# Second products of a routed feed-forward layer: 192 tokens as the moving side, the last 64 tokens summed from fetched rows

## The reference

```python
q = (xi @ w_query).reshape(B, T, PEER_HEADS, 2, PEER_HALF)
s = jnp.einsum('bthcd,cnd->bthcn', q, sub_keys)
s_top, i_top = lax.top_k(s, PEER_TOPK)          # 16 of 128, twice per head
...                                             # 16 best of the 256 pairs, softmax -> gate, idx
u = u_tab[idx]
h = gelu(einsum('bthk,btd->bthk', u, xi))
w = gate * h
return jnp.einsum('bthk,bthkd->btd', w, v_tab[idx])
```

## Time and profile before

| | |
|---|---|
| median of 3 runs | 2190.05 us (2189.86 to 2190.96) |
| the profiled execution | 2193.35 us, span 2191.6 us |
| TensorE (PE) busy | 2158.0 us, 98% |
| VectorE (DVE), ScalarE (ACT), POOL busy | 71%, 57%, 32% |
| memory read | 371.96 MB, 170 GB/s over the span |

### The profile page before, as it was taken

How to read it: one execution, slowest core, us unless ns; L and a number is a source line. 1 busy time by engine, 2 the same in 40 slices (tenths; PEclk the granted TensorE clock), 3 DMA queues, 4 the chain that set the end, 5 groups by cost and what they waited for, 6 DMA issues and landing times. The chain is left out here.

```text
span 2191.6 us, 35588 instructions
## 1 busy us (share of the span) xinstructions
PE 2158.0 (98%) x13179; PEld 1882.8 (86%) x13179; DVE 1558.1 (71%) x2948; ACT 1250.2 (57%) x2471; POOL 704.0 (32%) x344
## 2 busy tenths in 40 slices
PE   8899999999999999999999999999999999999999
PEld 8789998888888888887999888888888889897888
DVE  8558978888666666665698778866666668457776
ACT  6444567777554545564446777755555455555443
POOL 2217977777100000001698777730000004100000
PEclk9899999999999999999999999999999999999999
DMA  5144555555566665553555555556666656434554
GB/s 173 48 156 155 193 173 165 164 170 164 187 193 193 195 194 192 167 169 104 179 187 183 168 166 165 164 182 192 192 193 194 195 168 221 135 108 166 189 192 153
DMA packets 122956, 375.34 MB, mean 171 GB/s; under 512 B 13200, under 2 KB 18064, under 8 KB 122784
## 3 DMA queue, kind: packets, MB, share of 16 engines
q1 hardware_dynamic: 122496, 373.05, 52.8%
q10 hardware_dynamic: 288, 0.01, 0.0%
HBM read 371.96 MB, written 1.05 MB: 170 GB/s over the span
## 5 line engine op out<-in xcount | busy, mean ns | idle before, releaser
L250 ACT ACTIVATE hi<-raw 128x1024 fp32r<-128x1024 f32 (+2 forms) x705 | 738.0, 1048 | 361.4 <-PE bank L1439 114.1
L259 DVE TENSOR_TENSOR lo<-raw,hi 128x1024 fp32r<-128x1024 f32 (+2 forms) x449 | 544.5, 1216 | 262.1 <-ACT hi L250 261.6
L259 POOL TENSOR_TENSOR lo<-raw,hi 128x1024 fp32r<-128x1024 f32 x256 | 620.4, 2428 | 212.3 <-ACT hi L250 212.0
L1480 PE MATMUL bank<-hi,pe_mh 128*128 128x512 f32 x1016 | 395.7, 389 | 1.3 <-DVE pe_ml L1734 1.3
L1481 PE MATMUL bank<-hi,pe_ml 128*128 128x512 f32 x1016 | 395.3, 389 | 0.0
L1428 PE MATMUL bank<-xx,hi 128*128 128x512 f32 x1176 | 308.9, 401 | 0.0
L1593 ACT ACTIVATE pe_mh<-pe_hidden 128x256 fp32r<-128x256 f32 x256 | 106.9, 418 | 342.0 <-PE bank L1487 342.0
L342 POOL TENSOR_TENSOR rstd<-mean,minus_half 128x2 f32<-128x2 f32 x6 | 4.2, 704 | 902.9 <-DVE mean L335 902.9
L1439 PEld LDWEIGHTS bank<-xx,lo 128*128 128x128 f32 x2048 | 270.3, 189 | 14.0
L1439 PE MATMUL bank<-xx,lo 128*128 128x256 f32 x2048 | 281.4, 280 | 0.0
L1487 PE MATMUL bank<-lo,pe_mh 128*128 128x512 f32 x1016 | 271.5, 389 | 0.0
(11 more groups left out here) (418 smaller groups left out, 3408.6 us busy)
## 6 DMA issues: line engine op xcount, KB each, us to landing
raw<-in_peer_u SPq DMA_DIRECT2D x256, 512.0 KB, 3.3
raw<-in_peer_v SPq DMA_DIRECT2D x256, 512.0 KB, 4.3
raw<-in_w_gate_up SPq DMA_DIRECT2D x44, 512.0 KB, 3.6
raw<-in_w_in SPq DMA_DIRECT2D x34, 512.0 KB, 4.2
raw<-in_gla_w_in SPq DMA_DIRECT2D x24, 512.0 KB, 3.6
raw<-in_w_down SPq DMA_DIRECT2D x22, 512.0 KB, 3.4
raw<-in_w_query SPq DMA_DIRECT2D x16, 512.0 KB, 3.3
raw<-in_mla_w_o SPq DMA_DIRECT2D x8, 512.0 KB, 3.3
```

Source lines behind the costliest of these rows:

```text
L250: act.activation(k.hi[:, n % RING, at_hi:at_hi + x * e], k.raw[:, n % RAW, 0:x * e], ACT.Copy).then_inc(k.hi_done, 1)
L259: eng.tensor_tensor(k.lo[:, n % RING, at_lo:at_lo + x * e], k.raw[:, n % RAW, 0:x * e], k.hi[:, n % RING, at_hi:at_hi + x * e].bitcast(F32 ...
L1480: pe.matmul(second_ps(a, c), mh[:, v % 2, tok], hi[:, r, half], start=(v == 0), stop=False)
```

## The change

The 256 tokens are split: the first 192 (`TD`) go on as before through streamed slabs, the last 64 (`TS`) get their second weights by indirect fetch.

For the 192, the second products are turned. The slab is now the array's weights, 128 columns at a time, and the middle values move: for each of eight 128-wide pieces of the width, one product of 384 columns (high and low part of 192 tokens, side by side in `middle`) with the slab's high part, and one of 192 columns with its low part. The sums come out as width by tokens in all eight banks. At the end of the stage ScalarE takes each bank's low half out, VectorE adds it to the high half, TensorE transposes the sums back (16 transposes), and only then are they added to `h`.

For the 64, ScalarE writes their function values to `stage`, which SyncE stores to a table in memory (`aside`, 16 stores of 256 KB). VectorE's ranking also computes for each of their 128 picks the expert's row and the place in `aside`. In the second stage a token has two partitions, with 64 picks each. POOL issues two indirect fetches for a pick: 128 single values of `aside` (`seen`) and 128 rows of 4 KB of the second weights (`found`, four places). VectorE multiplies value and gate and adds the scaled rows to `sums_aside`, in the steps of `PICK_AT` (steps 10 to 108, 64 of them), and merges the two halves at step 115. The streams of both weight tables stay whole.

The groups for the gates are 48 instead of 64, at `LEAD + g * 7 // 5`. Some semaphores are shared under new names.

```diff
@@ -1271,7 +1271,13 @@
 
 
 GROUP = 4
-GROUPS = T // GROUP
+TS = 64
+TD = T - TS
+ASIDE = P // TS
+PICKS = SLOTS // ASIDE
+STAGED = 8
+FOUND = 4
+GROUPS = TD // GROUP
...
-    return LEAD + g * 5 // 4
-
-
+    return LEAD + g * 7 // 5
...
 V_ORDER = ((0, 0), (1, 0), (0, 1), (1, 1))
+V_BANK = (4, 5, 6, 7, 3, 2, 0, 1)
+PICK_AT = {10 + n * 25 // 16: n for n in range(PICKS)}
+MERGE_AT = 115
 GROUP_AT = {slab_of(g): g for g in range(GROUPS)}
...
                 for c in range(2):
                     sp.dma_start(keys[c * 64:(c + 1) * 64, c * NK:(c + 1) * NK],
                                  k.dram["sub_keys"][l, :, c, :]).then_inc(keyed.sem, 16)
+
+                def put_aside(b):
+
+                    sp.wait_ge(bent.sem, bent.at(STAGED * b + STAGED))
+                    sp.dma_start(aside[:, STAGED * b:STAGED * (b + 1), :], stage[:, b % 2])\
+                        .then_inc(written[b % 2].sem, 16)
+
+                def place_picks():
+
+                    sp.wait_ge(ranked.sem, ranked.at(2))
+                    for g in range(ASIDE):
+                        sp.dma_start(picks[g * TS:(g + 1) * TS], packed[P - TS:P, :, g * PICKS:(g + 1) * PICKS])\
+                            .then_inc(placed.sem, 16)
+
                 for n in range(s0 + AHEAD, end + AHEAD):
                     load_slab(k, sp, n)
+                    i = n - u0 - STAGED
+                    if i == TURN + 2:
+                        place_picks()
+                    if 0 <= i < NK and i % STAGED == STAGED - 1:
+                        put_aside(i // STAGED)
 
...
@@ -1468,39 +1523,50 @@
                                              start=(hot is hot_h), stop=(hot is hot_l))
                     last.then_inc(summed.sem, 1)
 
+                def high(v, c):
+
+                    cols = hi[:, (v0 + v) % RING, c * P:(c + 1) * P]
+                    pe.matmul(k.bank[V_BANK[c]][:, 0:2 * TD], cols, middle[:, v % 2].rearrange("p s t -> p (s t)"),
+                              start=(v == 0), stop=False, skip_group_check=True)
+
+                def low(v, c):
+
+                    return pe.matmul(low_sum(c), lo[:, (v0 + v) % RING, SKEW + c * P:SKEW + (c + 1) * P],
+                                     middle[:, v % 2, 0], start=False, stop=(v == NK - 1), skip_group_check=True)
+
                 def second(v):
 
-                    r = (v0 + v) % RING
                     pe.wait_ge(m_lo.sem, m_lo.at(v + 1))
                     pe.wait_ge(k.hi_done, v0 + v + 1)
-                    for c in range(2):
-                        half = slice(c * 512, (c + 1) * 512)
-                        for a in range(NT):
-                            tok = slice(a * P, (a + 1) * P)
-                            pe.matmul(second_ps(a, c), mh[:, v % 2, tok], hi[:, r, half], start=(v == 0), stop=False)
-                            pe.matmul(second_ps(a, c), ml[:, v % 2, tok], hi[:, r, half], start=False, stop=False)
-                    pe.wait_ge(*k.lo_at[v0 + v])
-                    for c in range(2):
-                        half = slice(c * 512, (c + 1) * 512)
-                        for a in range(NT):
-                            tok = slice(a * P, (a + 1) * P)
-                            last = pe.matmul(second_ps(a, c), mh[:, v % 2, tok], lo[:, r, half], start=False,
-                                             stop=(v == NK - 1))
+                    for part in (range(0, 5), range(5, KD)) if v == 0 else (range(KD),):
+                        for c in part:
+                            if v == 0 and V_BANK[c] < 3:
+                                pe.wait_ge(gated.sem, gated_before(NK - 1 - (NK - 1 - V_BANK[c]) % 3))
+                            high(v, c)
+                        pe.wait_ge(*k.lo_at[v0 + v])
+                        for c in part:
+                            last = low(v, c)
                     last.then_inc(k.eaten, 1)
 
                 def last_second():
 
                     v = NK - 1
-                    r = (v0 + v) % RING
                     pe.wait_ge(m_lo.sem, m_lo.at(v + 1))
                     pe.wait_ge(k.hi_done, v0 + v + 1)
                     pe.wait_ge(*k.lo_at[v0 + v])
-                    for n, (a, c) in enumerate(V_ORDER):
-                        half, tok = slice(c * 512, (c + 1) * 512), slice(a * P, (a + 1) * P)
-                        pe.matmul(second_ps(a, c), mh[:, v % 2, tok], hi[:, r, half], start=False, stop=False)
-                        pe.matmul(second_ps(a, c), ml[:, v % 2, tok], hi[:, r, half], start=False, stop=False)
-                        pe.matmul(second_ps(a, c), mh[:, v % 2, tok], lo[:, r, half], start=False, stop=True)\
-                          .then_inc((first_part.sem if n < 3 else k.eaten), 1)
+                    for c in range(KD):
+                        high(v, c)
+                        low(v, c).then_inc((joined.sem if c < KD - 1 else k.eaten), 1)
+
...
+
+                    for a, half in V_ORDER:
+                        pe.wait_ge(added.sem, added.at(4 * half + 4))
+                        tok = slice(a * P, min((a + 1) * P, TD))
+                        for x in range(4):
+                            last = pe.transpose(second_ps(a, half)[0:tok.stop - tok.start, x * P:(x + 1) * P],
+                                                sums_t[:, 4 * half + x, tok], k.ident[:])
+                        last.then_inc(returned.sem, 1)
 
...
+                turn_back()
...
+                pool.wait_ge(placed.sem, placed.at(16 * ASIDE))
+                for x in range(2):
+                    pool.wait_ge(written[x].sem, written[x].at(8 * NK // STAGED))
+                for n in range(PICKS):
+                    if n >= FOUND:
+                        pool.wait_ge(mixed.sem, mixed.at(n - FOUND + 1))
+                    pool.indirect_dma_start(seen[:, n:n + 1], None, aside.rearrange("j i t -> (j i t)").unsqueeze(1),
+                                            bass.IndirectOffsetOnAxis(ap=picks[:, 1, n:n + 1], axis=0))\
+                        .then_inc(picked[n % FOUND].sem, 16)
+                    pool.indirect_dma_start(found[:, n % FOUND], None, v_rows,
+                                            bass.IndirectOffsetOnAxis(ap=picks[:, 0, n:n + 1], axis=0),
+                                            element_offset=l * NK * NK * D)\
+                        .then_inc(picked[n % FOUND].sem, 16)
+                pool.wait_ge(mixed.sem, mixed.at(PICKS))
+                for g in range(ASIDE - 1):
+                    pool.dma_start(others[P - TS:P, g * D:(g + 1) * D], sums_aside[g * TS:(g + 1) * TS])\
+                        .then_inc(merged.sem, 16)
                 after.roots(pool)
...
+                    b = i // STAGED
+                    if b >= 2 and i % STAGED == 0:
+                        act.wait_ge(written[b % 2].sem, written[b % 2].at(16 * (b // 2)))
+                    last = act.activation(stage_of(i), made[:, TD:T], ACT.Gelu)
                     if cut:
                         last = act.activation(ps[:, 0:cut], made[:, 0:cut], ACT.Gelu)
-                    if cut < T:
-                        last = act.activation(hidden[:, i, cut:], made[:, cut:], ACT.Gelu)
+                    if cut < TD:
+                        last = act.activation(hidden[:, i, cut:], made[:, cut:TD], ACT.Gelu)
...
+                    act.activation(middle[:, v % 2, 0], hidden[:, v], ACT.Copy).then_inc(m_hi.sem, 1)
...
+                def keep_low_sum(c):
+
+                    if c < KD - 1:
+                        act.wait_ge(joined.sem, joined.at(c + 1))
+                    else:
+                        act.wait_ge(k.eaten, end)
+                    act.activation(low_sums[:, c], low_sum(c), ACT.Copy).then_inc(halved.sem, 1)
...
+                    row, col, gates = (x.rearrange("p g x -> p (g x)")
+                                       for x in (expert[:, 0, H_P:], expert[:, 1, H_P:], gate[:, H_P:]))
+                    ordered([dve.scalar_tensor_tensor(out=number[:, 0], in0=row, scalar=float(NK), in1=col, op0=ALU.mult,
+                                                      op1=ALU.add),
+                             dve.tensor_scalar(number[:, 1], row, float(TS), lane, ALU.mult, ALU.add)])
+                    ordered([dve.scalar_tensor_tensor(out=number[:, 1], in0=col, scalar=float(NK * TS), in1=number[:, 1],
+                                                      op0=ALU.mult, op1=ALU.add)])
+                    dve.tensor_copy(packed[:, 2].bitcast(F32), gates)
+                    dve.tensor_copy(packed[:, 0:2], number).then_inc(ranked.sem, 1)
                     dve.wait_ge(turned.sem, turned.at(1))
...
+                    dve.tensor_tensor(middle[:, v % 2, 1], hidden[:, v], middle[:, v % 2, 0].bitcast(F32), ALU.subtract)\
                         .then_inc(m_lo.sem, 1)
+
+                def mix(n):
+
+                    dve.wait_ge(picked[n % FOUND].sem, picked[n % FOUND].at(32 * (n // FOUND) + 32))
```

(30 more changed lines are left out.)

89 lines of the change are left out of this document (61 added, 28 removed).

## The result

The change makes the kernel faster: 2098.06 us median of 4 runs (2096.42 to 2099.76) against 2189.95 (2189.58 to 2190.96) on the same chip, a ratio of 0.958, interval [0.956, 0.960]. The prediction had 2123 us, 2103 to 2143 as the forecast's own band, and 2080 to 2215 as its whole range. The profiled execution took 2098.77 us, 94.6 less than that of before.

A forecast was written before the change was run, and what follows sets the result against it. TensorE's time was taken to bound the kernel. Per layer -16.8 - 12.5 - 8.2 + 4 = -33.5 us, -67 for two, took 2190.05 to 2123 us; own band 2103 to 2143, whole range 2080 to 2215.

The forecast's parts named there:

- rival (1): Second-weights stage: all else is covered and TensorE alone sets 2.29 us a pick step; 2072 us, chance 0.18.
- Products: Second-weights stage: eight 384-column products at 0.173 and eight 192-column at 0.113, 2.29 us a slab; 29 steps give -12.5 a layer.
- Pace of the 99 pick steps: Second-weights stage, steps 10 to 108: 2.55 us a step against 2.72 before, -16.8 us a layer.
- the bounds: Second-weights stage: DMA at 379 or 316 GB/s moves a pick step's 0.863 MB in 2.28 or 2.73 us.
- That rule's 2095 us: Second-weights stage: at the skill's 358 GB/s a core, a step takes 2.41 us and the kernel 2095 us.
- hidden: Second-weights stage: POOL's two fetches a pick cost nothing while both fit into 3.9 us, 1.97 a fetch.
- rival (3): Second-weights stage: POOL's fetches decide; at 2.4 us each 2204 us, slower; chance 0.22 with (4) and a worse DMA.
- Rival (4): Second-weights stage: VectorE slows POOL's fetches to 2.6 us at the upper end, 2255 us; 0.22 with (3) and worse DMA.
- First-weights stage: First-weights stage: 48 groups of one-hot products replace 64, 16 x 0.51 = -8.2 us a layer; ranking steps cost nothing.
- Start and end: Second-weights stage: +1 us in step 0 for the gate, +3 at the end for returning the sums; +4 a layer.
- Merge: Second-weights stage, step 115: two VectorE adds of 1.2 us, covered by 0.7 us to spare a step and three slabs; nothing.
- Nothing else moves: Rest of the kernel: no change beyond the summed terms of -33.5 us a layer, -67 for two.

The follow-up runs named there:

- 128 columns: Changed kernel with the products of a slab's low part moving 128 instead of 192 columns; 2096.63 us.
- 8-column sums: Changed kernel with each pick's scaled sum over 8 of its 1024 columns, all fetches kept; 2084.98 us.
- the kernel with pairs: Changed kernel with 56 of 64 picks, in pairs of neighbouring steps with two free steps behind each pair; 2105.41 us.
- the two kernels with 56 picks: Changed kernel with eight picks left out: one pick in every second step, 2088.48 us; pairs of neighbouring steps, 2105.41 us.
- the best: Changed kernel with small multiply on ScalarE, picks spread wider, and the merge's two adds in steps 121 and 124; 2081.72 us.

## Why the prediction was right, and where its size was off

- **The number.** 2098 lies in the stated range, but 5 us below the forecast's own band of 2103 to 2143: between it and rival (1), all covered, 2072. That rival's time is what the kernel without picks has (2071.77). So the way, the engine and the larger part of the gain were foreseen; the loss to the picks was put too high.
- **Products.** Right: 2.30 a step (forecast 2.29). The 384-column products are 1.43 / 8 = 0.179 apart (785.35 to 787.65 above), forecast 0.173; those of 192 are 0.87 / 8 = 0.109, forecast 0.113; the two errors cancel, which is luck. That the columns don't set the latter was shown with 128 columns.
- **Pace of the 99 pick steps: the mis-sized term.** "I take 2.55 us for the 99 steps: just over VectorE's 2.53" measured 2.40 and 2.39. That is 99 x 0.15 = 15 us a layer, 31 in all, where forecast and result are 25 apart. The other 6 went the other way: merges 2.4, the profiled run 0.7 above the median for the 3.3 reckoned with, and the small terms below. The failed step is the sum of VectorE's full durations, 2.53, where distances between starts count, 2.30; the engine was named rightly. The 0.10 above 2.30 is not mean load but order: pairs of picks, and late slabs. The working knew both sums and took the wrong one, with "three in-order limits at 2.3 to 2.5 seldom meet without a gap" as the reason; the gap is 0.10, not 0.26.
- **DMA.** 358 to 368 GB/s over 225 us at a share of 0.97 to 0.98, where the bounds were 379 and 316. The Trainium skill (DMA: Bandwidth & Descriptors, Specifications) has about 358 GB/s for a core; the run with 8-column sums is 3% above it. That rule's 2095 us is nearer the 2098 than the forecast, but not by its mechanism: without the rows' traffic the time falls by 2.2 us only, hardly clear of noise.
- **POOL.** Right: hidden, at 1.0 to 2.0 us a fetch, 3.4 a pick on the mean against 3.7 to spend. It was nearer than that sounds: rival (3) turns slower at 4.7 us a pick, and with 8-column sums POOL took 4.6 for a while and stopped TensorE once. Rival (4), VectorE shuts POOL out, falls: 1.36 us a fetch with 8-column sums, 1.39 with full ones. The tenth that the prediction read as agreeing with what it cites on the ports was measured on POOL's own passes. The trace before has no fetch, so it could not show this either way.
- **First-weights stage.** Forecast -8.2 a layer, measured -8.8 and -6.7. Groups cost 3.30 - 2.78 as before; the second layer has one slab of 5.21. It comes from the new ranking steps, forecast as "five small ones on VectorE in front of a wait that already stands there; nothing". They take 5.5 us (1127.03 to 1132.48), nearly all of it in two:

```profile
1127.23 2.42 DVE L1786 TENSOR_SCALAR pe_hidden<-pe_hidden 128x128 f32<-128x128 f32 x1
...
1130.01 2.35 DVE L1789 COPY pe_found<-pe_hidden 128x128 f32<-128x128 f32 x1
...
1139.30 0.22 PE L1522 MATMUL bank<-pe_hot_h,pe_hot_j 128*128 128x128 f16 x1 [1.75 <-ACT pe_hot_l L1670]
```

  The other three are at 0.28 or 0.29. The wait that they were to hide in was 2.22 us long before, in this layer:

```profile
1178.52 0.69 DVE L1684 COPY pe_slots<-bank 128x512 f32<-128x512 f32 x1 [2.22 <-PE bank L1455]
```

  In the first layer it was 5.26 us long, and nothing was lost. Why two small instructions take 2.4 us is open.
- **Start and end.** Forecast +4, measured 0.6 for step 0 (2.90 for 2.30) and 2.7 at the end (5.0 us from the last step's start to the residual's transposes, for 2.30): +3.3.
- **Merge.** Forecast "nothing", measured 1.2 us a layer. VectorE's two adds stand in its step 115, and the low middle part of step 118 comes behind them; TensorE's rows of steps 117 and 118:

```profile
826.42 1.03 PE L1534 MATMUL bank<-pe_middle,lo 128*128 128x192 f32 x8
828.48 1.68 PE L1529 MATMUL bank<-pe_middle,hi 128*128 128x384 f32 x8 [1.03 <-DVE pe_middle L1842]
```

  The prediction's "three slabs ahead" was true of the slabs, not of the middle values, which have two places. Split over two steps, it cost nearly nothing.
- **Nothing else moves.** Nearly right: +0.9 us over the rest. There the granted clock may play a part. Outside the long stages, where TensorE pauses, both kernels have a few stretches at the lower level of 1.2 GHz, some 25 us in all before and 27 after, but in other places. Between the two second-weights stages the kernel before has none and the changed one three. The first of them is in this row, with a clock of 0.73 on the mean of 6 us:

```profile
860.00:866.00 6.00, 6.00 (x39) 6.00 (x40) 6.00 (x14) 3.55 (x9) 0.17 (x1) 0.73 0.11 20
```

  Why a given pause brings one and another not is open.

## What to carry to other kernels

Sum an in-order engine by distances between starts, and then ask not only whether the mean fits but how far the engine may fall behind: here one extra of 1.39 us fitted in a step with 0.1 us to spare, its neighbour cost 0.46 (in the kernel with pairs), and the mean load (2.30 against 2.30, and 2.10 in the two kernels with 56 picks) told nothing of it. The allowance is found in the trace as the earliest point in the consumer's step at which the engine can start its next piece, which is set by the shared buffers (two middles) and by the order on the engine ahead of it (ScalarE's copy, then its high part). Cut side work into pieces that put the engine back by less than that allowance, don't put two that are larger than a step's spare time into neighbouring steps, and leave the last piece some steps ahead of what reads its result. Even so no kernel with all picks came down to 2.30: the best still loses 0.03 us a step, to pairs (steps of 2.35 and 2.38) and to late slabs.

## What the hardware showed that was not expected

- A single core moved 368 GB/s on average over 225 us (8-column sums), with over a third of it (31.7 of 82.8 MB) in fetches that POOL issued.
- An indirect fetch of 128 rows holds POOL for 0.94 to 2.01 us, mostly near one end or the other, whether the rows are 4 bytes or 4 KB. In the first layer of the changed kernel 33 of the 35 behind a wait take about 2 us. But with 8-column sums 12 of 14 behind a wait take about 1, and eleven in a row without any wait take 2.0. So the wait alone does not decide it.
- A step whose first product had to wait takes 0.08 us more itself, after a wait of 0.38 as after one of 0.04 (2.68 and then 2.38 with picks in pairs, 2.34 and then 2.39 with one in every second step).
